# Shared expert's up and down products moved one turn earlier in a streamed mixture-of-experts step

## The reference

```python
def swiglu(x, w_gate, w_up, w_down):
    return (jax.nn.silu(x @ w_gate) * (x @ w_up)) @ w_down

# moe_ffn: 64 experts, TOP_K = 6 for each token, EXPERT_FF = SHARED_FF = 256
scores = jax.nn.sigmoid((x @ lw['router_w']).astype(jnp.float32))
...
routed = moe_dispatch(x, eidx, gates, lw['exp_w_gate'], lw['exp_w_up'], lw['exp_w_down'])
shared = swiglu(x, lw['sh_w_gate'], lw['sh_w_up'], lw['sh_w_down'])
return (routed + shared).reshape(B, L, D)
```

## Time and profile before

| | |
|---|---|
| median of 3 runs | 1327.57 us (1327.25 to 1329.88) |
| the profiled execution | 1327.29 us, of which the span of its instructions is 1325.4 us |
| PE busy | 1220.9 us, 92% of the span |
| DVE, ACT, POOL busy | 280.4, 239.4, 2.8 us |
| moved by DMA | 496.60 MB, mean 375 GB/s over the span |
| mean granted clock of TensorE | 0.968 of full speed |

### The profile page before, as it was taken

The page is one execution under the profiler, slowest core; times in us unless marked ns, Lnnn a source line. Parts: engine busy times, 40 slices in busy tenths (PEclk is TensorE's granted clock), DMA queues, the critical chain, the costliest instruction groups (busy, mean ns, idle before and its releaser), DMA issues.

```text
span 1325.4 us, 22620 instructions
## 1 busy us (share of the span) xinstructions
PE 1220.9 (92%) x9596; PEld 834.4 (63%) x9596; DVE 280.4 (21%) x720; ACT 239.4 (18%) x533; POOL 2.8 (0%) x13
## 2 busy tenths in 40 slices
PE   6999999998998898889999999999899898889896
PEld 4566687666765465546565658766667565556564
DVE  1252362110011010111034425401010110011012
ACT  2363132110010110011034421411010110011002
POOL 0000000000000000000000000000000000000000
PEclk9999999999999898889999999999999998889899
DMA  9879849999999999999966663999999999999993
GB/s 386 335 316 350 340 184 420 404 423 413 428 424 426 424 428 427 426 424 424 419 229 257 246 235 144 422 415 424 427 408 423 423 430 424 427 424 429 423 420 135
DMA packets 65684, 496.60 MB, mean 375 GB/s; under 512 B 8912, under 2 KB 11216, under 8 KB 23120
## 3 DMA queue, kind: packets, MB, share of 16 engines
q1 hardware_dynamic: 61552, 493.62, 90.0%
q10 hardware_dynamic: 4064, 2.00, 0.5%
HBM read 493.60 MB, written 2.00 MB: 374 GB/s over the span
## 4 chain that ended last, share of the span: by engine, by line
PE 54%; DMA 36%; SPq 3%; DVE 3%; issue 2%; ACT 1%; DVEq 0%; ACTq 0%
DMA gu<-in_exp_w_both 35%; PE PS L2231 17%; PE PS L1735 7%; PE PS L2067 4%; PE PS L2158 4%; PE PS L2267 4%; PE PS L2165 3%; PE PS L1677 2%; PE PS L1645 1%; DMA gu<-in_w_in 1%; PE PS L2116 1%; SPq L624 1%; SPq L627 1%; PE PS L1858 1%; PE PS L1869 1%
## 5 line engine op out<-in xcount | busy, mean ns | idle before, releaser
L2231 PE MATMUL PS<-gu,arena 128*32 128x256 f32 (+1 forms) x2848 | 237.5, 416 | 65.0 <-DMA gu<-in_exp_w_both 65.0
L2231 PEld LDWEIGHTS PS<-gu,arena 128*32 128x32 f32 (+1 forms) x2848 | 131.7, 124 | 158.8 <-DMA gu<-in_exp_w_both 72.3
L2158 PE MATMUL PS<-arena 128*128 128x128 f32 x1408 | 176.3, 278 | 0.5 <-ACT arena L1067 0.5
L2158 PEld LDWEIGHTS PS<-arena 128*128 128x128 f32 x1408 | 164.0, 192 | 17.8 <-issue 16.7
L2231 PE MATMUL PS<-arena 128*64 128x256 f32 x704 | 159.9, 386 | 8.9 <-DMA gu<-in_exp_w_both 8.9
L2165 PE MATMUL PS<-arena 128*128 128x256 f32 x704 | 160.2, 380 | 1.4 <-ACT arena L1050 1.4
L2267 PE MATMUL PS<-dn,arena 128*32 128x512 f32 (+1 forms) x688 | 160.2, 596 | 0.0
L2267 PE MATMUL PS<-arena 128*64 128x512 f32 (+1 forms) x336 | 152.6, 597 | 2.3 <-DVE arena L1550 1.6
L2165 PEld LDWEIGHTS PS<-arena 128*128 128x128 f32 x704 | 130.2, 190 | 20.5 <-ACT arena L1050 3.2
L2231 PEld LDWEIGHTS PS<-arena 128*64 128x64 f32 x704 | 96.0, 139 | 67.8 <-issue 19.0
L1556 DVE TENSOR_TENSOR arena<-arena,PS 128x256 f32<-128x256 f32 x44 | 18.5, 421 | 554.6 <-ACT arena L1063 554.6
(11 more groups left out here) (264 smaller groups left out, 1023.8 us busy)
## 6 DMA issues: line engine op xcount, KB each, us to landing
gu<-in_exp_w_both SPq DMA_DIRECT2D x72, 2048.0 KB, 20.6
dn<-in_exp_w_down SPq DMA_DIRECT2D x86, 1024.0 KB, 26.2
arena<-in_exp_w_down SPq DMA_DIRECT2D x42, 1024.0 KB, 27.0
gu<-in_w_ada SPq DMA_DIRECT2D x20, 2048.0 KB, 9.1
arena<-in_exp_w_both SPq DMA_DIRECT2D x20, 2048.0 KB, 23.5
gu<-in_exp_w_both SPq DMA_DIRECT2D x34, 1024.0 KB, 19.4
xh<-in_exp_w_both SPq DMA_DIRECT2D x12, 2048.0 KB, 36.1
gu<-in_w_in SPq DMA_DIRECT2D x8, 2048.0 KB, 14.9
```

Of the source, the lines that this page charges most:

```text
L2158: ins = mmul(PS[:, 4, (c % 4) * P:(c % 4) * P + P], h_tok[:, g, c], onehot[b][:, g], start=(g == 0), stop=(g == 1))
L2231: ins = mmul(PS[w * h:w * h + w, 5, FF * half:FF * half + FF], xg[:, k, w * h:w * h + w], weights[half][:, k], start=(k == 0), stop=(k == ...
```

## The change

Two constants move the shared expert's products one turn ahead each: `shared_up` from the pair round of turn 1 to that of turn 0, and `shared_down` from the pair round of turn 2 to that of turn 1.

```diff
-UP_TURN, DOWN_TURN = 1, 2
+UP_TURN, DOWN_TURN = 0, 1
```

## The result

| | before | after |
|---|---|---|
| median of the runs side by side | 1328.55 us (4 runs) | 1340.76 us (1339.45 to 1341.52, 4 runs) |
| ratio, 95% interval | | 1.0095 (1.0079 to 1.0112) |
| span of the profiled execution | 1325.4 us | 1338.8 us |
| PE busy | 1220.9 us | 1223.7 us |

The change costs 0.95%, 13.4 us of span. Predicted were 1327.9 us and no measurable change, with 1331.2 as the upper end of the range. The prediction was wrong: it forecast a change of 0.6 us that can't be told from none, and the measured time lies 9.6 us above the upper end of its range.

A forecast was written before the change was run, and what follows sets the result against it. The prediction took the DMA queue to bound the expert rounds. Its terms +1.8, -0.7 and -0.5 summed to +0.6 us on 1327.29, so 1327.9 us, with a range of 1324.7 to 1331.2.

The forecast's parts named there:

- What bounds the kernel: Expert rounds: the DMA queue at 425 GB/s is the bound; PE has some 6 us to spare in each turn.
- rival 4: PE's loop, one more iteration in each layer: its jump may need missing code, 0.83 us a block, 1329.6 us; chance 0.03.
- Less written code: Written turns: with one of three gone, a third of their DMA rate losses is saved, -0.5 us, bounds 0 and 1.55.
- The rule of the skill: Loop's jump: a taken branch to a page not held forces a fetch; the loop's rows were said not to show it.
- The lead at turn 0's pair: End of turn 0's pair: time from SP's issue to the previous load's landing shrinks to 1.9 us, costing 0.9 a layer, +1.8.
- the three prices: Losses read from the trace before: 0 at lead 2.6, 0.7 at 2.3, 1.2 at 1.7 us, said to form a line.
- The pair of turn 1: Turn 1's pair: its 3.54 us wait goes, its end moves to 329.4, lead 3.3; layer 1 saves its 0.7 us.
- Turn 2: Turn 2: PE loses shared_down, 6.9 us, and turn 3's quad then waits 3 to 6 us for gu weights.
- Rivals 1 to 3: Slower, queue dry after turn 0's pair, 1331.7 (0.14); faster, PE's waits real, 1320.2 (0.05); faster, written-turn losses gone, 1325.0 (0.10).

The follow-up runs named there:

- e1: Changed kernel with PE's turn 2 written out again ahead of its loop, six iterations as before; 1329.45 us, ratio 1.0016.
- e4: Kernel before with only shared_up moved (turn 1 to turn 0), shared_down left in turn 2; 1330.35 us, ratio 1.0019.
- e7: Changed kernel without PE's jump and overflow code behind the last quad; 1327.83 us, ratio 1.0003.
- e6: Kernel before with 72 instructions of satisfied waits added on PE just ahead of layer 0's loop; 1341.13 us, ratio 1.0095.
- e5: Changed kernel with 110 instructions of satisfied waits added on PE just ahead of layer 0's loop; 1331.03 us, ratio 1.0027.

## Why the prediction was wrong, by its own steps

**What bounds the kernel.** "PE has some 6 us to spare in each turn, and a wait of PE costs nothing as long as it doesn't make SP issue so late that the queue runs out." True in the turns (the waits for `gu` from 410 to 640 are still 30.8 us, 31.7 before), but I carried it over to the stage's end, where it doesn't hold. The last pair waits for no load: before, its gates followed the quad's down products with no gap (652.78 in the chain above). From there to the next layer's rounds PE's work is the bound, and a stop at this place goes to the end in full: the shift of 0.7 ahead of it has become 8.1 at the start of layer 1's rounds (848.38 before, 856.50 now).

**The step that failed: rival 4, and with it "Less written code".** Taking out a written turn was counted as a gain only, -0.5 us. The one rival that asked about code fetch was given 0.03 and a price of 0.83 us a block, 1329.6 us in all. Three things were wrong in it. It looked at the loop's jump back, whose rows show no wait, and not at the one jump behind the removed code, which is forward. It took the trace of before as evidence about the jump, when that trace can only show the place at which the jump stood before; that the change shifts all of PE's code behind it by 696 instructions a layer, 184 over two blocks, was never put into a term. And it priced a block by the share of its transfer. Of a stop, the transfer is 1.1 us (655.41 to 656.50 for the changed kernel's in layer 0), but PE stands for 4.41 and 4.22 us and then works at a granted clock of 0.50, together 7.4 and 5.7 us. With the measured price and the right place this rival gives 1327.3 + 13.1 = 1340.4, and 1340.76 was measured.

**The rule of the skill.** I wrote that the loop's rows "don't bear it out here". The rule was right, and there was a taken branch that it spoke of. I had tested it against a branch that the change leaves alone.

**The lead at turn 0's pair (+1.8).** Right in mechanism, a little small in size. The issue came at 285.35, with the load ahead landed at 287.2, a lead of 1.9. The 1 MB landed 4.0 behind its forerunner, where 2.5 is its own time: 1.5 us lost in layer 0, and by the same reckoning in layer 1 (issued at 933.78, landed 5.6 later at 939.4, the one ahead at 936.1) 0.8. Together 2.3 instead of 1.8, within the bounds. The lead in layer 1 was 2.3 and not 1.9. The price came from a line that the three prices don't fall on: from 0 at 2.6 to 1.2 at 1.7 it gives 0.4 at 2.3, where 0.7 stood in the trace of before and 0.8 stands now. The rate of 419 instead of 423 (1.3 us) fits the loss in layer 0.

**The pair of turn 1 (-0.7).** Its wait vanished as forecast (0.34 left) and its end came at 329.26 for the forecast 329.4, with no loss at its lead of about 4 us (3.3 was forecast). The shift of -0.4 between the two layers' stops is of the right sign. How much of it belongs to this term isn't separated.

**Turn 2.** As forecast: the quad of turn 3 waits 5.66, in the range of 3 to 6 us, and the time that PE gained went there.

**"Less written code", -0.5.** Nothing of it is seen: 419 and 420 GB/s in the same stretches with one written turn less, against 423 and 420. e1, which writes the turn out again, moves 419 in both.

**The sum of these.** Forecast +0.6 with the -0.5, +1.1 without it. The changed kernel's trace has +0.3, and e1 and e4, which move the loads without the stops, 0.16 and 0.19%, about 2 to 2.5 us. Which of these is nearer the truth isn't settled. Rivals 1 to 3 didn't occur. No version beat the kernel before: with the cause removed (e7, 1.0003) the change is worth nothing, which agrees with the prediction's reason, that a wait of PE is only turned into another one while the queue is the bound.

## What to carry to other kernels

A change that adds or removes code moves every jump behind it: list the taken jumps of the bounding engine, forward ones over rarely used paths above all, and give each a possible stop of the size seen here (3.5 to 4.6 us, with the slow clock behind it 5.4 to 7.4), if it stands where no wait for a transfer hides it. A trace without such a stop shows only that the jump stood well, not that it is free; when two versions differ by some microseconds at one jump with "issue" as the releaser, test with padding ahead of it or without the jump before anything else is believed. And ask of every "PE has time to spare" up to which round it holds.

## What the hardware showed that I had not expected

- A stop behind a forward jump over 327 instructions, in eight of the sixteen places seen in the eight kernels that have it: 4.1 to 4.6 us in five, 3.5 and 3.6 in two where a few gates still ran, 1.7 in one where the block was already on its way when PE came to the jump.
- A loss of the same 0.95% comes from 72 instructions that do nothing in an otherwise unchanged kernel (e6), and 110 of them take most of it away again (e5).
- 92 instructions of satisfied waits on PE took about 9 us at the start of the program, 72 took 6.8: near 0.1 us each.
- Each stop of 3.5 us or more came with a granted clock of 0.50 around its end or behind it. After the one of 1.71 us the clock stayed at 1.00 and the gates took 3.67.
- Behind a jump whose target is near its block's end, PE still runs one weight load (target at 238) or four gates (237) and stops only then.
